# The output gate's projection of linear attention as a section of its own ahead of the mLSTM's fill

## The chip, the cores and the metric

The kernel runs on one core of a Trainium2 chip. The metric is the device time of one launch in microseconds; lower is better. The core has five engines with a queue each: TensorE (PE in the profile), VectorE (DVE), ScalarE (ACT), GpSimd (POOL) and SyncE (SP, which only issues transfers here).

## What is computed

Two layers act on a residual stream of 512 positions and 1024 features. Each layer adds half a SwiGLU, then a mixer of three parallel token mixers, then half a SwiGLU.

```python
z = h @ w_in + b_in                        # all projections of the mixer
o_a = gla_chunked(a_q, a_k, a_v, log_alpha)            # gated linear attention
o_a = rms_norm(o_a, gla_out_norm) * silu(a_r)          # a_r: its output gate
o_b = nsa_attention(b_q, ...)                          # sparse attention, 8 heads
o_c = mlstm_chunked(c_q, c_k, c_v, c_i, log_f) * sigmoid(c_o)
y = (sigmoid(gate_a) * (o_a @ w_branch[0]) + sigmoid(gate_b) * (o_b @ w_branch[1])
     + sigmoid(gate_c) * (o_c @ w_branch[2]))
x = x + y @ w_out
```

The change is about where the four tiles of `a_r` (128 features by 512 positions each) are projected.

## The kernel before

**Tiles, units, steps.** Activations lie with features on the partitions and the 512 positions along the free axis. Every float32 weight goes through three passes: a transfer on SP brings a unit (two weight tiles) into `raw`; ACT copies a tile rounded into `whi` (line 298, `split_tile`; line 289 in loops); POOL subtracts to get the rest into `wlo` (line 265). PE then does three matmuls for each 128 input features: `hhi,whi`, `hlo,whi`, `hhi,wlo`. These three are called a step here. A projection tile has 8 steps (lines 1191 to 1193), a tile of a combine unit 6 (lines 1247 to 1249). `whi` and `wlo` have two places, so that tile T+2 is split once PE has ended tile T. Semaphores carry it: `tile_done`, `hi_done`, `lo_done`, `raw_ready`, and `unit_free` for the PSUM banks.

**Sections and fills.** `SECTIONS` gives the order of the weights. The three token mixers have long chains of small operations on ACT and DVE. While these run, PE gets steps of a section that needs no result of theirs. A plan is a pair: at how many steps each slot begins, and at how many steps each tile ends. On PE `fill_group(n)` or `fill(name, n)` emits the steps of slot n. On ACT and DVE `fill` and `fill_group`/`fill_combine` stand at their own places n and handle the tiles that end at or before slot n (`ended`): ACT splits tile T+2 and, in a combine unit, makes the gate with a sigmoid (line 412, which needs another activation table than the exponentials do); DVE adds a bias (line 793) or multiplies the gate in (line 803), which also frees the unit's banks. All three engines take their queues in order.

**Sparse attention** has 16 groups m: `values(m)` ends group m; `scores(m + 1)` stands ahead of its slots. Group m works on m mod 4 + 1 blocks of 128 columns and has four slots q. In each, PE transposes a row of probabilities (line 1458), ACT copies it out of the one bank 6 into `prt` (line 504) and makes the exponentials of the next group (line 492), and PE's next transposes wait for that copy. The fill is plan `PM1`: 12 tiles, 96 steps, 16 of them in slots 0 to 3, 80 in the 64 slots of the groups: one step in slots q = 0, 1, 2 and two in q = 3.

**mLSTM** first has a head of eight slots (0 to 7): PE transposes eight tiles (line 1288), DVE does the gates' scans and four convolutions of four operations each (lines 1013 and 1016), ACT copies and applies Silu (lines 525 and 528). Line 1484 waits for the last Silu. Then come four heads h with slots 8 + 4h to 11 + 4h: PE makes four products, slots 8 + 4h and 9 + 4h, three products (lines 1495 to 1497), slot 10 + 4h, the sums (lines 1501, 1504), slot 11 + 4h. Line 1488 of the next head waits for DVE's chain behind line 1504 (`h_out`, line 1050, behind a reciprocal). The fill is plan `CB` on section `cb0`: 16 tiles of 6 steps, 96 steps, four in each slot. Linear attention comes after that with `cb1`.

## Time and profile before

| | us |
|---|---|
| median of 3 runs | 2916.95 |
| lowest and highest | 2909.89, 2918.77 |
| the profiled execution's own time | 2915.71 |
| its span, first to last instruction | 2913.9 |
| PE busy | 2749.6 (94%) |
| DVE busy | 1304.5 (45%) |
| POOL busy | 1069.6 (37%) |
| ACT busy | 1024.4 (35%) |
| mean granted PE clock, of full speed | 0.979 |

Busy times of matmuls overlap a little, as they are pipelined, so PE's share is not its distance from its peak. Most of PE's waits lie where the three token mixers run. The stretches of interest are, in layer 0, 587 to 722 us (the sparse attention's groups), 722 to 758 (the mLSTM's head) and 758 to 849 (its four heads), and in layer 1 the same some 1442 us later.

### The profile page before, as it was taken

Reading aid. Unit: us, or ns where it says so; the run is one execution under the profiler, and the core shown is the slowest. Engines: PE = TensorE matmul, PEld = TensorE weight load, DVE = VectorE, ACT = ScalarE, POOL = GpSimd, SP = SyncE. Lnnn points to the kernel's source line nnn. Section 1 sums busy time; section 2 is a strip of 40 time slices with the busy share of each in tenths; the row PEclk is TensorE's granted clock in tenths of the full one; section 3 lists DMA queues with packets and bytes.
Section 4 is the critical chain, followed back from the end, with each engine's and each line's share of the span. In section 5 each row is a group of like instructions: output and inputs, shape, how many; then the busy total and the mean of one; then the engine's idle time right before and its main releaser. Section 6 shows DMA issues by size and latency. Waiting matters only on the chain.

```text
span 2913.9 us, 36798 instructions
## 1 busy us (share of the span) xinstructions
PE 2749.6 (94%) x13092; PEld 2169.3 (74%) x13092; DVE 1304.5 (45%) x1596; ACT 1024.4 (35%) x1498; POOL 1069.6 (37%) x450
## 2 busy tenths in 40 slices
PE   6999999999988999999999999999998889999998
PEld 5888877766666787888878888767665667878887
DVE  6333353444655455332353333444454563653322
ACT  3222233555535433222232222244554454332221
POOL 3444444411222343444434444443112223444443
PEclk9999999999989999999999999999998999999999
DMA  3222222211111132223222222232011112222231
GB/s 134 89 99 103 99 87 97 100 45 34 53 45 44 66 108 92 88 100 114 89 73 101 96 100 92 87 108 87 30 44 44 55 44 76 101 92 99 88 119 68
DMA packets 36070, 239.54 MB, mean 82 GB/s; under 512 B 3952, under 2 KB 5232, under 8 KB 13936
## 3 DMA queue, kind: packets, MB, share of 16 engines
q1 hardware_dynamic: 32720, 232.80, 22.7%
q10 hardware_dynamic: 3232, 5.17, 0.5%
q8 instruction: 74, 1.21, 0.2%
q14 instruction: 44, 0.36, 0.0%
HBM read 234.81 MB, written 2.10 MB: 81 GB/s over the span
## 4 chain that ended last, share of the span: by engine, by line
issue 63%; POOL 24%; PE 11%; POOLq 1%; DVE 0%; DVEq 0%
POOL wlo L265 24%; PE bank L1191 4%; PE bank L1192 4%; PE bank L1193 4%; POOLq L264 1%; POOLq L260 1%; DVE hlo L689 0%; DVE x L759 0%; POOL selr L252 0%; DVE hhi L687 0%; POOLq L265 0%; POOLq L256 0%; POOL ones L249 0%; POOL onesm L250 0%; DVEq L759 0%
## 5 line engine op out<-in xcount | busy, mean ns | idle before, releaser
L265 POOL TENSOR_TENSOR wlo<-raw,whi 128x1024 fp32r<-128x1024 f32 (+2 forms) x440 | 1068.0, 2429 | 1825.2 <-ACT whi L298 926.1
L1191 PE MATMUL bank<-hhi,whi 128*128 128x512 f32 x1984 | 798.4, 402 | 48.3 <-POOL wlo L265 36.7
L1193 PE MATMUL bank<-hhi,wlo 128*128 128x512 f32 x1984 | 777.8, 392 | 0.0
L1192 PE MATMUL bank<-hlo,whi 128*128 128x512 f32 x1984 | 777.5, 392 | 0.0
L289 ACT ACTIVATE whi<-raw 128x1024 fp32r<-128x1024 f32 (+1 forms) x232 | 264.0, 1138 | 717.8 <-PE bank L1193 717.6
L1191 PEld LDWEIGHTS bank<-hhi,whi 128*128 128x128 f32 x1984 | 376.4, 190 | 137.9 <-issue 47.2
L1193 PEld LDWEIGHTS bank<-hhi,wlo 128*128 128x128 f32 x1984 | 375.5, 189 | 79.5
L1192 PEld LDWEIGHTS bank<-hlo,whi 128*128 128x128 f32 x1984 | 376.3, 190 | 75.0 <-issue 3.1
L746 DVE TENSOR_TENSOR tmp<-tmp,bank 128x512 f32<-128x512 f32 x80 | 55.0, 688 | 534.0 <-PE bank L1193 534.0
L1191 PE MATMUL bank<-uhi,whi 128*128 128x512 f32 x704 | 274.3, 390 | 0.0
L1193 PE MATMUL bank<-uhi,wlo 128*128 128x512 f32 x704 | 273.9, 389 | 0.0
L1192 PE MATMUL bank<-ulo,whi 128*128 128x512 f32 x704 | 273.9, 389 | 0.0
L298 ACT ACTIVATE whi<-raw 128x1024 fp32r<-128x1024 f32 (+2 forms) x176 | 173.2, 987 | 278.3 <-PE bank L1193 138.8
L736 DVE TENSOR_TENSOR ulo<-tmp,uhi 128x512 f32 (+1 forms) x88 | 212.6, 2415 | 10.1
L1247 PE MATMUL bank<-hhi,whi 128*128 128x512 f32 x384 | 165.9, 432 | 16.8 <-POOL wlo L265 16.6
L386 ACT ACTIVATE tmp<-bank 128x512 f32<-128x512 f32 x80 | 47.8, 597 | 362.1 <-PE bank L1193 347.8
L759 DVE SCALAR_TENSOR_TENSOR x<-bank,x 128x512 f32 x32 | 22.1, 692 | 319.2 <-PE bank L1193 319.2
L1248 PE MATMUL bank<-hlo,whi 128*128 128x512 f32 x384 | 156.3, 407 | 0.0
L689 DVE SCALAR_TENSOR_TENSOR hlo<-x,cur,hhi x48 | 153.5, 3198 | 6.2
L1249 PE MATMUL bank<-hhi,wlo 128*128 128x512 f32 x384 | 155.3, 404 | 0.0
L1191 PEld LDWEIGHTS bank<-uhi,whi 128*128 128x128 f32 x704 | 132.2, 188 | 28.6 <-issue 1.2
L1193 PEld LDWEIGHTS bank<-uhi,wlo 128*128 128x128 f32 x704 | 132.2, 188 | 27.7
(266 smaller groups left out, 3148.9 us busy)
## 6 DMA issues: line engine op xcount, KB each, us to landing
raw<-gu SPq DMA_DIRECT2D x88, 1024.0 KB, 4.8
raw<-dn SPq DMA_DIRECT2D x32, 1408.0 KB, 6.0
raw<-cb SPq DMA_DIRECT2D x48, 768.0 KB, 4.3
raw<-pM SPq DMA_DIRECT2D x16, 1024.0 KB, 4.7
raw<-cq SPq DMA_DIRECT2D x16, 1024.0 KB, 4.8
raw<-pA SPq DMA_DIRECT2D x12, 1024.0 KB, 4.7
raw<-wo SPq DMA_DIRECT2D x8, 1024.0 KB, 4.8
x<-xT ACTq DMA_DIRECT2D x4, 512.0 KB, 9.7
```

The lines of the kernel that those rows point to most:

```text
L265: pool.tensor_tensor(wlo[:, s, 0:w], raw[:, j, lo:lo + w], whi[:, s, 0:w].bitcast(f32), ALU.subtract).then_inc(sem["lo_done"], 1)
L289: A(whi[:, s, 0:w], raw[:, j, lo:lo + w], ACT.Copy).then_inc(sem["hi_done"], 1)
L298: A(whi[:, s, 0:(wa, wb)[s]], raw[:, u % 2, s * wa:s * wa + (wa, wb)[s]], ACT.Copy).then_inc(sem["hi_done"], 1)
L689: dve.scalar_tensor_tensor(hlo[:, c], x[:, c], gain, hhi[:, c].bitcast(f32), ALU.mult, ALU.subtract).then_inc(sem["pre_lo"], 1)
L736: dve.tensor_tensor(ulo[:, c], tmp[:, 2 + j], uhi[:, c].bitcast(f32), ALU.subtract).then_inc(sem["ulo_ready"], 1)
L746: dve.tensor_tensor(tmp[:, 2 + j], tmp[:, j], bank[2 * j + 1][:], ALU.mult).then_inc(sem["unit_free"], 1)
L1191: mm(outp, wh, mhi, start=start and k == 0, stop=False)
L1192: mm(outp, wh, mlo, start=False, stop=False)
L1193: i = mm(outp, wl, mhi, start=False, stop=stop and k == len(parts) - 1)
L1247: mm(outp, wh, mhi, start=k == (2 if s else 0), stop=False)
L1248: mm(outp, wh, mlo, start=False, stop=False)
L1249: i = mm(outp, wl, mhi, start=False, stop=bool(s) and k in (1, 5))
```

## The change

The last four of the twelve tiles of `pM1`, which are `a_r`, become section `pR`. The order of weights on SP, ACT and POOL is as it was. The sparse attention's 64 slots get 48 steps in place of 80: none in q = 0, one in q = 1, 2, 3. The mLSTM's 24 slots get 128 steps (four tiles of 8, then `cb0`'s sixteen of 6), 5 or 6 in each slot, in place of 96. No arithmetic is added or taken away.

```diff
-SECTIONS = [..., ("pM0", 2), ("cq", 8), ("pM1", 6), ("cb0", KD), ("cb1", KD),
+SECTIONS = [..., ("pM0", 2), ("cq", 8), ("pM1", 4), ("pR", 2), ("cb0", KD), ("cb1", KD),
...
-PM1 = ([4 * n if n < 4 else 16 + (n - 4) * 80 // 64 for n in range(69)], [KD * (i + 1) for i in range(12)])
+PM1 = ([4 * n if n < 4 else 16 + (n - 4) * 48 // 64 for n in range(69)], [KD * (i + 1) for i in range(8)])
+RCB = ([n * 128 // 24 for n in range(25)], [KD * (i + 1) for i in range(4)] + [4 * KD + 6 * (i + 1) for i in range(2 * KD)])
...
 # ACT: RCB's tiles
+                def fill_first(n):
+                    for T in ended(RCB, n):
+                        if T + 2 < len(RCB[1]):
+                            split_tile("pR", T + 2)
+                        if T >= 4 and T % 2:
+                            gate_unit(0)(T - 4)
...
-                split_tile("cb0", 0)
-                split_tile("cb0", 1)
+                split_tile("pR", 0)
+                split_tile("pR", 1)
...
-                    fill("cb0", CB, n, gate_unit(0))
+                    fill_first(n)
...
                 for h in range(NH):
                     fill("cb1", CB, h, gate_unit(1))
+                act.wait_ge(sem["unit_free"], me.at("unit_free", FIRST["pR"] + 2))
...
 # DVE
+                def fill_first(n):
+                    for T in ended(RCB, n):
+                        if T < 4:
+                            group_tile(FIRST["pR"] + T // 2, T % 2, MT_TILES - 4 + T)
+                        elif T % 2:
+                            combine_unit(0, T // 2 % 2, FIRST["cb0"] + T // 2 - 2, T // 2 - 2)
...
 # PE
+                def fill_first(n):
+                    at, ends = RCB
+                    for c in range(at[n], at[n + 1]):
+                        T = min(i for i, e in enumerate(ends) if c < e)
+                        u, s = FIRST["pR"] + T // 2, T % 2
+                        free = u - 1 if s == 0 else None
+                        if T < 4:
+                            step(2 * u, s, bank[2 * (u % 2) + s][:], hp, c % KD, free=free)
+                        else:
+                            gated(2 * u, u % 2, s, (c - 4 * KD) % 6, free=free)
...
-                        fill("cb0", n - 1)
+                        fill_first(n - 1)
...
-    arr["pM0"], arr["pM1"] = pm[:, 0:2], pm[:, 6:12]
+    arr["pM0"], arr["pM1"], arr["pR"] = pm[:, 0:2], pm[:, 6:10], pm[:, 10:12]
```

On PE, in the sparse attention's second group (two blocks), the first slot stood as follows: two transposes, a step, then the next two transposes and a step.

```order
L1458 MATMUL bank<-con,tmp 128x128 x2
L1191 MATMUL bank<-hhi,whi 128x512
L1192 MATMUL bank<-hlo,whi 128x512
L1193 MATMUL bank<-hhi,wlo 128x512
L1454 REGISTER_ALU
L1458 MATMUL bank<-con,tmp 128x128 x2
L1191 MATMUL bank<-hhi,whi 128x512
L1192 MATMUL bank<-hlo,whi 128x512
L1193 MATMUL bank<-hhi,wlo 128x512
```

With the change (its lines are numbered a little higher: 1488 is what was 1458, and 1209 to 1211 what was 1191 to 1193) the same place reads:

```order
L1488 MATMUL bank<-con,tmp 128x128 x2
L1484 REGISTER_ALU
L1488 MATMUL bank<-con,tmp 128x128 x2
L1209 MATMUL bank<-hhi,whi 128x512
L1210 MATMUL bank<-hlo,whi 128x512
L1211 MATMUL bank<-hhi,wlo 128x512
```

The first slot's step has gone, so that the second pair of transposes follows the first pair with nothing between. The last slot of the same group stood so, with two steps ahead of the values (line 1439):

```order
L1458 MATMUL bank<-con,tmp 128x128 x2
L1375 REGISTER_ALU
L1186 REGISTER_ALU
L1191 MATMUL bank<-hhi,whi 128x512
L1192 MATMUL bank<-hlo,whi 128x512
L1193 MATMUL bank<-hhi,wlo 128x512
L1191 MATMUL bank<-hhi,whi 128x512
L1192 MATMUL bank<-hlo,whi 128x512
L1193 MATMUL bank<-hhi,wlo 128x512
L1439 MATMUL bank<-prt,raw 64x128 x8
L1442 MATMUL bank<-tmp,vcm 64x128 x2
```

It now has one step there:

```order
L1488 MATMUL bank<-con,tmp 128x128 x2
L1209 MATMUL bank<-hhi,whi 128x512
L1210 MATMUL bank<-hlo,whi 128x512
L1211 MATMUL bank<-hhi,wlo 128x512
L1469 MATMUL bank<-prt,raw 64x128 x8
L1472 MATMUL bank<-tmp,vcm 64x128 x2
```

On DVE, in the mLSTM's head, the first convolution stood behind one multiplication of a gate (line 803), which reads PSUM:

```order
L1004 TENSOR_SCALAR zm<-zm 128x512
L1005 REGISTER_ALU
L802 REGISTER_ALU
L803 TENSOR_TENSOR y<-tmp,bank 128x512
L805 REGISTER_ALU
L1013 TENSOR_SCALAR tmp<-zm,cur 128x512
L1014 REGISTER_ALU
L1016 SCALAR_TENSOR_TENSOR tmp<-zm,cur,tmp 128x511
```

Now two bias additions stand there (line 794 is what was 793, 1031 and 1034 what was 1013 and 1016):

```order
L1022 TENSOR_SCALAR zm<-zm 128x512
L1023 REGISTER_ALU
L793 REGISTER_ALU
L794 TENSOR_SCALAR zm<-bank,cur 128x512
L793 REGISTER_ALU
L794 TENSOR_SCALAR zm<-bank,cur 128x512
L1031 TENSOR_SCALAR tmp<-zm,cur 128x512
L1032 REGISTER_ALU
L1034 SCALAR_TENSOR_TENSOR tmp<-zm,cur,tmp 128x511
```

One more addition stands behind the second convolution and one behind the third, where one multiplication stood behind the third. The multiplications move to the four heads.

## Rows read from the trace of the kernel before

**Rows 1.** Busy time by stretch (us; PE, PEld, DVE, ACT, POOL; granted clock, DMA share, GB/s).

```profile
587.20:722.30 135.10, 130.99 (x958) 89.20 (x956) 63.77 (x142) 69.62 (x197) 23.35 (x11) 0.99 0.11 36
722.30:757.80 35.50, 29.08 (x135) 22.18 (x133) 30.64 (x37) 19.97 (x28) 10.04 (x5) 0.95 0.20 67
757.80:782.00 24.20, 22.40 (x74) 14.90 (x74) 9.47 (x14) 14.67 (x23) 7.28 (x4) 0.86 0.10 33
782.00:842.00 60.00, 56.58 (x196) 38.88 (x196) 25.92 (x39) 21.78 (x38) 10.95 (x6) 0.89 0.16 53
```

**Rows 2.** What PE waited for, both layers (total us, times, longest).

```profile
PE bank L1488 <- DVE tmp L1050: 10.4, 6, 1.8
...
PE bank L1458 <- ACT prt L504: 6.4, 10, 1.0
```

**Rows 3.** Timeline of ACT in the sparse attention (start us, us long, instruction).

```profile
650.10 0.60 ACT L504 ACTIVATE prt<-bank 128x512 f32<-128x512 f32 x1 [0.46 <-PE bank L1458]
...
664.93 0.20 ACT L492 ACTIVATION_READ_ACCUMULATOR tmp<-bank,st 128x1 f32 x1
665.16 0.38 ACT L504 ACTIVATE prt<-bank 128x256 f32<-128x256 f32 x1
```

**Rows 4.** Timeline of PE in the sparse attention.

```profile
657.68 0.30 PE L1458 MATMUL bank<-con,tmp 128*128 128x128 f32 x1 [0.96 <-ACT prt L504]
...
664.71 0.41 PE L1458 MATMUL bank<-con,tmp 128*128 128x128 f32 x2
...
665.69 0.41 PE L1458 MATMUL bank<-con,tmp 128*128 128x128 f32 x2
...
667.49 0.77 PE L1439 MATMUL bank<-prt,raw 128*64 128x128 f32 x10
```

**Rows 5.** Timeline of PE, mLSTM of layer 0.

```profile
757.79 0.49 PE L1484 MATMUL bank<-rows,selr 64*128 64x512 f32 x1 [1.82 <-ACT zm L528]
...
768.79 0.91 PE L1495 MATMUL bank<-zm 64*128 64x384 f32 x2
...
770.29 0.50 PE L1247 MATMUL bank<-hhi,whi 128*128 128x512 f32 x1
...
773.14 2.32 PE L1501 MATMUL bank<-raw,zm 128*128 128x512 f32 x8
...
781.95 0.49 PE L1488 MATMUL bank<-rows,selr 64*128 64x512 f32 x1 [1.80 <-DVE tmp L1050]
```

**Rows 6.** Timeline of PE, mLSTM of layer 1.

```profile
2200.18 0.79 PE L1484 MATMUL bank<-rows,selr 64*128 64x512 f32 x1 [3.43 <-ACT zm L528]
...
2212.59 0.91 PE L1495 MATMUL bank<-zm 64*128 64x384 f32 x2
```

**Rows 7.** Timeline of DVE in the mLSTM of layer 0.

```profile
737.12 2.07 DVE L1004 TENSOR_SCALAR zm<-zm 128x512 f32<-128x512 f32 x1
...
739.84 0.42 DVE L1004 TENSOR_SCALAR zm<-zm 128x512 f32<-128x512 f32 x1
740.38 0.69 DVE L803 TENSOR_TENSOR y<-tmp,bank 128x512 f32<-128x512 f32 x1
...
741.81 2.32 DVE L1016 SCALAR_TENSOR_TENSOR tmp<-zm,cur,tmp 128x511 f32<-128x511 f32 x3
...
744.75 3.74 DVE L1016 SCALAR_TENSOR_TENSOR tmp<-zm,cur,tmp 128x511 f32<-128x511 f32 x3
...
772.65 0.69 DVE L803 TENSOR_TENSOR y<-tmp,bank 128x512 f32<-128x512 f32 x1
```

**Rows 8.** Timeline of POOL in the mLSTM of layer 0.

```profile
736.54 2.37 POOL L265 TENSOR_TENSOR wlo<-raw,whi 128x768 fp32r<-128x768 f32 x1 [2.73 <-ACT whi L298]
...
762.05 1.82 POOL L265 TENSOR_TENSOR wlo<-raw,whi 128x768 fp32r<-128x768 f32 x1 [10.25 <-ACT whi L298]
```

**Rows 9.** Timeline of ACT in the mLSTM of layer 0.

```profile
761.14 0.83 ACT L298 ACTIVATE whi<-raw 128x768 fp32r<-128x768 f32 x1
...
765.36 0.64 ACT L548 ACTIVATE tmp<-bank 128x512 f32<-128x512 f32 x1
```

More of the change, by code:

```diff
@@ L26 @@
 R_F, R_I, R_LR, R_G = 0, 32, 64, 96
-SECTIONS = [("gu0", KF), ("dn0", KD), ("pA", 6), ("pM0", 2), ("cq", 8), ("pM1", 6), ("cb0", KD), ("cb1", KD),
+SECTIONS = [("gu0", KF), ("dn0", KD), ("pA", 6), ("pM0", 2), ("cq", 8), ("pM1", 4), ("pR", 2), ("cb0", KD), ("cb1", KD),
             ("cb2", KD), ("wo", KD // 2), ("gu1", KF), ("dn1", KD)]
@@ L191, in build @@
             "cs_mm": 2, "cs_sub": 2, "cs_exp": 2, "cs_out": 2, "cs_t": 2, "cs_pt": 2,
-            "s_mm": 64, "s_max": 32, "s_exp": 64, "s_p": 64, "s_t": 64, "s_pt": 64, "pv": 16, "g_free": 12,
+            "s_mm": 64, "s_max": 32, "s_exp": 64, "s_p": 64, "s_t": 64, "s_pt": 64, "pv": 16, "g_free": 8,
             "o_hi": 12, "o_lo": 12,
@@ L293, in split_tile @@
                     u, s = FIRST[name] + T // 2, T % 2
-                    wa, wb = widths(name)
+                    wa, wb = widths(name) if name != "pR" or T < 4 else widths("cb0")
                     if s == 0:
@@ L532, in _ @@
                 for h in range(NH):
-                    fill("cb0", CB, 8 + 4 * h, gate_unit(0))
+                    fill_first(8 + 4 * h)
                     if h:
@@ L549, in _ @@
                     for n in range(1, 4):
-                        fill("cb0", CB, 8 + 4 * h + n, gate_unit(0))
-                fill("cb0", CB, 24, gate_unit(0))
+                        fill_first(8 + 4 * h + n)
+                fill_first(24)
                 split_tile("cb1", 0)
@@ L790, in fill_group @@
                     for T in ended(PM1, n):
-                        u, c = FIRST["pM1"] + T // 2, MT_TILES - 12 + T
+                        c = MT_TILES - 12 + T
                         dve.wait_ge(sem["tile_done"], me.at("tile_done", 2 * FIRST["pM1"] + T + 1))
@@ L1007, in _ @@
                 for n in range(4):
-                    fill_combine(0, n)
+                    fill_first(n)
                 for c in range(4):
@@ L1018, in _ @@
                         dve.wait_ge(sem["cv"], me.next("cv"))
-                    fill_combine(0, 4 + c)
+                    fill_first(4 + c)
                 dve.wait_ge(sem["rt_mm"], me.next("rt_mm"))
@@ L1022, in _ @@
                 for h in range(NH):
-                    fill_combine(0, 8 + 4 * h)
+                    fill_first(8 + 4 * h)
                     dve.wait_ge(sem["d_exp"], me.next("d_exp"))
@@ L1038, in _ @@
                     dve.wait_ge(sem["den_sum"], me.next("den_sum"))
-                    fill_combine(0, 9 + 4 * h)
-                    fill_combine(0, 10 + 4 * h)
+                    fill_first(9 + 4 * h)
+                    fill_first(10 + 4 * h)
                     dve.wait_ge(sem["den_mm"], me.next("den_mm"))
@@ L1054, in _ @@
                     dve.wait_ge(sem["h_gated"], me.next("h_gated"))
-                    fill_combine(0, 11 + 4 * h)
-                fill_combine(0, 24)
+                    fill_first(11 + 4 * h)
+                fill_first(24)
                 def out_low(b, first, tiles=range(4)):
@@ L1475, in _ @@
                 i.then_inc(sem["rt_mm"], 1)
-                fill("cb0", 7)
+                fill_first(7)
                 pe.wait_ge(sem["vm_ready"], me.at("vm_ready", 8))
@@ L1490, in _ @@
                     mm(bank[6][:], sel(h), rows[:, 1], start=True, stop=True).then_inc(sem["mm_mm"], 1)
-                    fill("cb0", 8 + 4 * h)
-                    fill("cb0", 9 + 4 * h)
+                    fill_first(8 + 4 * h)
+                    fill_first(9 + 4 * h)
                     pe.wait_ge(sem["d_exp"], me.next("d_exp"))
@@ L1497, in _ @@
                     mm(bank[4][:, 2 * P:3 * P], k[:, 3 * P:S], q[:, 3 * P:S], start=True, stop=True).then_inc(sem["sm_mm"], 1)
-                    fill("cb0", 10 + 4 * h)
+                    fill_first(10 + 4 * h)
                     for jt in range(NB):
@@ L1504, in _ @@
                     mm(bank[6][:], ones[:], tmp[:, 4], start=True, stop=True).then_inc(sem["den_mm"], 1)
-                    fill("cb0", 11 + 4 * h)
+                    fill_first(11 + 4 * h)
                 fill("cb1", 0)
```

## The prediction

> **What bounds the kernel now.** The page gives PE 94% of the span, so I looked for the stretches in which PE is not what ends last. The busy times by stretch show three of them [rows 1]. In the sparse attention PE is busy 130.99 of 135.10 us at a granted clock of 0.99. In the mLSTM's head it is busy 29.08 of 35.50 us; DVE, with 30.64 us, is the denser engine there. In the four heads PE is busy nearly throughout, but the granted clock is 0.86 and 0.89 of full speed. So the step that looks best placed today is one in the sparse attention, and the one that looks free is one in the mLSTM. The timelines say something else about the first.
>
> In the sparse attention I looked at ACT behind PE's transposes. ACT ends reading its accumulator at 665.13 and starts its next copy at 665.16 [rows 3]: it has no gap. PE's transposes follow each other in the same 0.98 us, from 664.71 to 665.69, with one step between [rows 4]. So slots q = 0 to 2 run at ACT's pace. The slot with two steps takes 1.80 us, from 665.69 to 667.49, 0.82 more [rows 4]; there PE ends last. With four blocks ACT falls idle for 0.46 us and then copies for 0.60 [rows 3]; PE's next transposes wait for that copy, which takes as long as the step does.
>
> In the mLSTM I looked at what PE waits for. Line 1488 waits for DVE's reciprocal chain 10.4 us in six waits [rows 2], 1.80 of them ahead of the second head [rows 5]. Line 1484 waits for DVE's convolutions through ACT's last Silu, 1.82 us in layer 0 and 3.43 in layer 1 [rows 5, 6]: DVE's chain, not PE's work, sets where the head ends.
>
> **Price of a step.** Four steps take 2.85 us, from 770.29 to 773.14 [rows 5], with some 0.12 of drain; another one beside them costs 0.68. The change takes 32 steps, 21.9 us a layer, from one place and puts them in the other. Transfers, splits and subtractions stay in their order on SP, ACT and POOL.
>
> **The sparse attention, a layer.** The 16 steps of q = 0 lie under ACT's work [rows 3, 4]: taking them away gives 0. With one block the copy is short and PE's next transposes could start a little sooner, but ACT's exponentials would still hold the ones after. The second step of q = 3 is worth 0.68, bounded above by the 0.82 of the two-step slot. With four blocks ACT's last copy then comes a little after the step, and I count 0.55. Twelve times 0.68 and four times 0.55 are 10.4. What could be late next is DVE's scaling of the next group; the values and scores stand between, and the copies are all that PE waits for there now [rows 2]. Then the splits: where ACT splits a weight between two copies, PE waits, 0.96 us in one case [rows 4] and 6.4 us in ten over both layers [rows 2]. By the plan six of eight splits a layer fall between copies; after it two of four. Of 3.2 us a layer, two waits of 0.85 stay: gain 1.5. Sum: -11.9 a layer, -23.8 for both.
>
> **The mLSTM's head, a layer.** Ten more steps, 6.8 us, enter the eight slots, in which PE is now idle for 6.4 us [rows 1]. The end is DVE's. It loses two multiplications (0.69 each [rows 7]) and gets four bias additions that read PSUM too; at the same 0.69 that is +1.4. POOL decides the rest. While POOL subtracts from 736.54 to 738.91 [rows 8], DVE's line 1004 takes 2.07 us, elsewhere 0.42; three operations of line 1016 take 3.74 in place of 2.32 [rows 7]. The passes move: if line 1004 is no longer hit, the head ends 1.65 earlier (-0.3); if one more operation is hit, 1.65 later (+3.0). I take +1.3. The Trainium skill, "SBUF — State Buffer", section "SBUF: two separate sides", says that DVE and GpSimd share a pair of ports as an exclusive lock for a whole instruction. The stretched line 1004 agrees; by that rule the head's bound is set by whose instruction starts first, which no sum foretells.
>
> **First head.** ACT does four sigmoids, then the split. It ends 761.97 [rows 9] and POOL 763.87 [rows 8], 6.1 us after line 1484. Now that tile begins two steps into slot 8 in place of four, so PE waits for it: a wait of 0.7 to 2.4 us by the clock. Six steps later comes the next tile, whose split stands behind the exponentials: ACT ends them at 766.00 [rows 9], 8.2 after line 1484; 0.83 and 1.82 more [rows 8, 9] are 11.1. Three more steps end at 13.2. Before, line 1495 stood 11.0 behind line 1484 in layer 0 [rows 5] and 12.4 in layer 1 [rows 6]. So +2.2 and +0.8. Slot 10 has one step more (0.68), and its fourth begins the third combine unit, whose banks DVE frees only behind line 803, 4.55 us after line 1495 [rows 5, 7]. PE is there at 3.6: a new wait of 1.0. That is +1.7 in each layer. Slot 11's two extra steps lie under the 1.80 that line 1488 waits.
>
> **Later heads.** Heads 1 to 3 get 12 steps a layer that nothing covers, 8.2 us, and one each in slots 15 and 19 that the wait covers. The waits at line 1488 shrink from 1.80 to 0.4, 1.1 and 1.1. The granted clock was 0.89 over these 60 us [rows 1]; a clock at either 1.2 or 2.4 GHz makes that 13.2 us at 1.2, which cost 6.6. I take it that PE's shorter waits no longer bring it down: -6.6. Net +1.6. The last slot's two steps lie under DVE's work for linear attention; I put 0.4 on it.
>
> **Sum.** Layer 0: 1.3 + 2.2 + 1.7 + 1.6 + 0.4 = 7.2. Layer 1: 5.8. Together +13.0, against -23.8: -10.8 us. The profiled execution took 2915.71, 1.2 below the median of 2916.95. From 2915.7 this gives 2904.9, from the median 2906.2. I say 2905.
>
> **Rivals.**
> - *The clock keeps falling between heads*, chance 0.17. For it: it fell behind waits of 1.8 us with PE at work on both sides. Against it: the waits shrink by 0.7 to 1.4. Price 6.6 a layer: 2918, no change. The Trainium skill, "TensorE: Matmul & The Clock Gate", section on HAM oscillation, tells of kernels in which a wait ahead of each block of work puts the clock down each time. The granted 0.89 here agrees; by that rule, if 1.1 us is still enough, the time is this rival's.
> - *DVE's chain in the head gets off lightly*, 0.15. Line 1004 is not hit (-1.6 a layer), PE hardly waits at line 1484 and the clock in the first head, 0.86 over 24.2 us [rows 1], comes back to full, 3.4 us at most, about half of it behind the new wait for the split. That is about -7 more: 2898.
> - *Supply of weights*, 0.12. Tiles now follow each other with less other work between, and splits stand behind ACT's exponentials in each head. If the third and fourth head wait like the first, 2 us and the clock's 1.7 for two heads and both layers give +15 at worst, +7 likely: 2912. In the third head the tile is needed about 6.0 us behind line 1488 and I find it ready at 5.2; that is close.
> - *The other side: the second step of q = 3 is covered as well*, 0.07. If what follows it (values, scores, the next first transposes) is really held by ACT's exponentials and DVE's scaling, then only 3.0 of the splits come back against +13.0: 2926, slower. The kernel ends slower at all once less than half of the 10.4 is won, and by over 0.3% only if next to nothing of it is. Against it: the two-step slot is 0.82 longer than its neighbours.
> - The forecast, 0.49, with its own range of 2899 to 2910.
>
> **Numbers.** A measurement of this kernel tells about 0.3%, 8.7 us, from no change: faster is below 2908. The forecast gives 0.41 of its chance to faster and 0.08 to same; the light chain 0.15 faster; the clock 0.14 same and 0.03 slower; supply 0.04 faster, 0.07 same, 0.01 slower; the other side 0.07 slower. Sum 0.60, 0.29, 0.11. The range 2894 to 2918 reaches to the light chain below and to the middle of the clock's case above.
>
> **What would show it.** Right: slots of q = 3 at about 1.1 us and q = 0 to 2 as before; the sparse attention's 135.1 us at about 123; line 1484 within 1 to 3 us of its old distance from the first transposes; line 1488 waiting 0.4 to 1.1; a clock near 1.0 over heads 1 to 3; new waits for POOL in slot 8 and for DVE in slot 10 of the first head. Wrong: q = 0 slots that get shorter, a clock that stays at 0.89, or waits for `wlo` in every head.

## The result and the profile after

The changed kernel takes 2919.05 us in the median of ten runs (2912.86 to 2922.51); the kernel before, run ten times beside it, 2911.36. The ratio is 1.0026 with a 95% interval of 1.0014 to 1.0038: some 7.7 us slower, where 10.8 us faster was forecast. (The median of 2916.95 that the forecast started from was that of three runs; ten runs of the same kernel spread from 2903.74 to 2918.77.) The profiled execution took 2918.60 us over a span of 2916.8. Two single executions in the slow state, of 15,378 us (the kernel before, beside e5, e6 and e7) and of 11,066 us (e9), count in no ratio.

The four stretches that answer to [rows 1], in layer 0 of the kernel after (the columns are those of [rows 1]):

```profile
585.90:710.20 124.30, 112.29 (x862) 74.81 (x860) 63.27 (x138) 65.83 (x192) 13.22 (x6) 0.97 0.07 26
710.20:749.20 39.00, 35.19 (x166) 28.04 (x162) 34.56 (x39) 16.07 (x24) 12.80 (x6) 0.96 0.18 61
749.20:777.30 28.10, 24.27 (x92) 16.03 (x91) 9.39 (x13) 15.84 (x25) 9.13 (x5) 1.00 0.18 57
777.30:842.40 65.10, 63.06 (x237) 45.01 (x238) 27.36 (x41) 25.12 (x42) 16.45 (x9) 0.95 0.17 61
```

The sparse attention, 135.10 us before, takes 124.30. The head is 3.5 us longer, with DVE at 34.56 us in place of 30.64. The clock is back in the first head (1.00 for 0.86), but only at 0.95 in the later ones. What PE waited for, both layers, beside [rows 2]:

```profile
PE bank L1488 <- ACT prt L513: 11.1, 17, 0.8
PE bank L1318 <- ACT zm L534: 5.7, 2, 2.9
PE bank L1518 <- DVE tmp L1068: 4.9, 6, 1.1
PE bank L1265 <- DVE y L813: 1.5, 2, 0.8
```

Line 1518 (1488 before) waits 4.9 us in place of 10.4; line 1318 (1288) has a wait of 2.9 us in each layer for ACT's copy, and the wait for DVE's line 813 is new.

All kernels of this study, by the starts of the same matmuls in their timelines, layer 0 / layer 1, in us. "Sparse" runs from the first transposes (line 1458 before) to the product for alpha (line 1451), which stands ahead of the last group; "head" from there to line 1484, so that it holds the sparse attention's last group too; "four heads" to the last head's line 1501; "LA 2nd half" is linear attention's second pair of heads, in which no kernel changes anything. The time is the median; each ratio goes by runs of the kernel before beside that kernel.

| kernel | steps in the mLSTM | sparse | head | four heads | LA 2nd half | time | ratio to before |
|---|---|---|---|---|---|---|---|
| before | 96 | 124.9 / 125.7 | 45.7 / 45.6 | 81.6 / 83.0 | 45.1 / 45.2 | 2911.4 | |
| after | 128 | 113.6 / 113.8 | 49.8 / 49.8 | 90.5 / 90.6 | 48.0 / 48.0 | 2919.1 | 1.0026 |
| e1, narrow passes | 128 | 113.9 / 113.5 | 46.0 / 46.0 | 88.5 / 87.0 | 48.1 / 48.1 | 2905.0 | 0.9979 [0.9967, 0.9990] |
| e2, waits covered | 128 | 113.7 / 113.7 | 49.8 / 49.8 | 83.5 / 83.5 | 48.1 / 48.1 | 2905.6 | 0.9978 [0.9965, 0.9991] |
| e3, one unit, even | 112 | 116.6 / 116.4 | 48.7 / 48.3 | 82.8 / 82.3 | 47.9 / 48.2 | 2906.1 | 0.9983 [0.9971, 0.9996] |
| e4, one unit, placed | 112 | 117.2 / 116.3 | 48.5 / 48.4 | 74.0 / 74.0 | 47.8 / 45.9 | 2888.4 | 0.9921 [0.9900, 0.9942] |
| e5, two units, placed | 128 | 114.0 / 113.5 | 52.8 / 52.8 | 80.1 / 80.1 | 47.9 / 45.5 | 2898.6 | 0.9956 [0.9941, 0.9971] |
| e6, none moved, placed | 96 | 125.6 / 124.9 | 46.7 / 46.6 | 69.8 / 71.4 | 48.1 / 45.2 | 2891.9 | 0.9928 [0.9913, 0.9944] |
| e8, as e4, splits last | 112 | 111.3 / 111.5 | 47.7 / 47.5 | 74.0 / 74.6 | 45.9 / 48.1 | 2877.5 | 0.9873 [0.9854, 0.9892] |
| e9, as e8, head changed | 112 | 112.2 / 111.4 | 51.1 / 50.5 | 75.8 / 75.4 | 47.5 / 48.2 | 2885.4 | 0.9896 [0.9877, 0.9916] |
| e10, two units, splits last | 128 | 112.0 / 112.6 | 52.9 / 52.9 | 83.3 / 82.0 | 47.2 / 45.5 | 2902.9 | 0.9972 [0.9959, 0.9985] |
| e11, as e6, splits last | 96 | 118.7 / 118.7 | 48.8 / 48.8 | 71.4 / 71.4 | 47.6 / 47.5 | 2882.6 | 0.9899 [0.9880, 0.9918] |

Against before, the kernel after wins 11.4 and 12.0 us in the sparse attention and loses 4.1 and 4.1 in the head (0.6 of it in the sparse attention's last group, 3.5 behind it), 8.9 and 7.6 in the four heads, 1.4 and 1.4 from there to linear attention, and 2.9 and 2.9 in linear attention's second half. The first question was why the head and the heads cost more than forecast, the second where the last 2.9 come from.

DVE in the head of the kernel after, and POOL beside it:

```profile
711.72 2.65 DVE L994 SCALAR_TENSOR_TENSOR tmp<-z 4x512 f32<-4x512 f32 x1
...
724.48 3.30 DVE L1017 TENSOR_TENSOR rows<-tmp,rows 4x1024 fp32r<-4x1024 f32 x1
...
731.35 1.56 DVE L1031 TENSOR_SCALAR tmp<-zm,cur 128x512 f32<-128x512 f32 x1
...
735.89 3.79 DVE L1034 SCALAR_TENSOR_TENSOR tmp<-zm,cur,tmp 128x511 f32<-128x511 f32 x3
...
741.04 3.79 DVE L1034 SCALAR_TENSOR_TENSOR tmp<-zm,cur,tmp 128x511 f32<-128x511 f32 x3
```

```profile
709.12 4.71 POOL L266 TENSOR_TENSOR wlo<-raw,whi 128x1024 fp32r<-128x1024 f32 x2 [37.37 <-ACT whi L299]
724.27 2.42 POOL L266 TENSOR_TENSOR wlo<-raw,whi 128x1024 fp32r<-128x1024 f32 x1 [10.44 <-ACT whi L299]
730.22 2.41 POOL L266 TENSOR_TENSOR wlo<-raw,whi 128x1024 fp32r<-128x1024 f32 x1 [3.53 <-ACT whi L299]
736.75 2.38 POOL L266 TENSOR_TENSOR wlo<-raw,whi 128x768 fp32r<-128x768 f32 x1 [4.12 <-ACT whi L299]
```

The first three long instructions of DVE start inside one of POOL's passes and end 0.3 to 1.1 us behind it. Line 1017 works on four partitions; it starts 0.21 us behind the start of POOL's pass of 724.27 and ends 1.09 behind its end, so that of its 3.30 us some 2.2 are the rest of the pass. Twice a pass falls into the three operations of a convolution, which then take 3.79 in place of 2.32, as in [rows 7]. Line 1004, which took 2.07 us there, is not hit now.

PE in the same place has one long wait at the head's start and none at its end:

```profile
718.82 0.66 PE L1318 MATMUL bank<-con,zm 128*128 128x128 f32 x4 [2.88 <-ACT zm L534]
...
749.24 0.49 PE L1514 MATMUL bank<-rows,selr 64*128 64x512 f32 x1
```

```profile
748.56 0.63 ACT L537 ACTIVATE zm<-tmp 128x512 f32<-128x512 f32 x1 [2.57 <-DVE tmp L1034]
```

ACT's last Silu ends at 749.19, and PE is busy up to line 1514 at 749.24: both end together, where PE had waited 1.82 us before [rows 5].

### The profile page after: what moved, and what is told of

It is laid out like the page before. It is cut to its first block, busy times and chain, and to the rows that moved or that the text cites. A ratio compares the mean times of both kernels' runs of the same rounds, so it can differ in the third digit from the quotient of the medians.

```text
span 2916.8 us, 36796 instructions
## 1 busy us (share of the span) xinstructions
PE 2741.5 (94%) x13092; PEld 2168.2 (74%) x13092; DVE 1313.8 (45%) x1596; ACT 1018.0 (35%) x1492; POOL 1072.4 (37%) x450
## 3 DMA queue, kind: packets, MB, share of 16 engines
q8 instruction: 74, 1.21, 0.2%
## 4 chain that ended last, share of the span: by engine, by line
issue 63%; POOL 24%; PE 11%; POOLq 1%; DVE 0%; DVEq 0%
POOL wlo L266 24%; PE bank L1209 4%; PE bank L1211 4%; PE bank L1210 4%; POOLq L265 1%; POOLq L261 1%; DVE hlo L699 0%; DVE x L769 0%; POOL selr L253 0%; DVE hhi L697 0%; POOLq L266 0%; POOLq L257 0%; POOL ones L250 0%; POOL onesm L251 0%; DVEq L769 0%
## 5 line engine op out<-in xcount | busy, mean ns | idle before, releaser
L1209 PEld LDWEIGHTS bank<-hhi,whi 128*128 128x128 f32 x1984 | 376.3, 190 | 139.9 <-issue 48.4
L387 ACT ACTIVATE tmp<-bank 128x512 f32<-128x512 f32 x80 | 47.9, 599 | 357.3 <-PE bank L1211 343.1
L1210 PEld LDWEIGHTS bank<-ulo,whi 128*128 128x128 f32 x704 | 132.2, 188 | 27.5
```

Of the source, the lines that this page charges most:

```text
L1209: mm(outp, wh, mhi, start=start and k == 0, stop=False)
L1210: mm(outp, wh, mlo, start=False, stop=False)
```

## The experiments

**e1: is the head longer because of POOL's passes?**

```diff
-                                pool.tensor_tensor(wlo[:, s, 0:w], raw[:, j, lo:lo + w],
-                                                   whi[:, s, 0:w].bitcast(f32), ALU.subtract).then_inc(sem["lo_done"], 1)
+                                n_ = 64 if name == "pR" else w
+                                pool.tensor_tensor(wlo[:, s, 0:n_], raw[:, j, lo:lo + n_],
+                                                   whi[:, s, 0:n_].bitcast(f32), ALU.subtract).then_inc(sem["lo_done"], 1)
```

> The kernel after, in which GpSimd's subtraction for the four tiles of the output gate works on 64 columns only (the rest of wlo of these tiles is left out, so part of the projection's correction is missing); everything else stays. Theory A, the mLSTM's head is longer by 4.1 us a layer because VectorE's operations (the 2.65, 3.30 and 1.56 us that stood at 0.73, 1.22 and 0.55 before) lie under GpSimd's longer passes: these three operations fall back to their short times, the 2.88 us wait for ACT's copy of zm shrinks by 2 us or more and the low clock behind it goes; the head gets 3 to 4.5 us shorter in each layer, and the whole kernel 6 to 9 us faster than the kernel after, about level with the kernel before. Rival B, the head is longer because TensorE has ten more steps in it and is itself the bound: the operations may get shorter, but the distance from line 1484's matmul of alpha to line 1514 changes by less than 1 us, and so does the time.

DVE in the same place (lines stand one lower):

```profile
712.32 0.67 DVE L995 SCALAR_TENSOR_TENSOR tmp<-z 4x512 f32<-4x512 f32 x1
...
723.14 1.21 DVE L1018 TENSOR_TENSOR rows<-tmp,rows 4x1024 fp32r<-4x1024 f32 x1
...
730.86 0.55 DVE L1032 TENSOR_SCALAR tmp<-zm,cur 128x512 f32<-128x512 f32 x1
731.45 2.32 DVE L1035 SCALAR_TENSOR_TENSOR tmp<-zm,cur,tmp 128x511 f32<-128x511 f32 x3
```

The three operations fall to 0.67, 1.21 and 0.54 to 0.55 us, and the head from 49.8 to 46.0 in both layers, with the same 42 steps in it. PE's wait of 2.9 us for ACT's copy is 0.89 now, and the low clock that followed it (3.4 us at half the clock, so 1.7 us lost) is gone. These two make up the 3.8 us. The wait hangs on the first of the three operations alone, the one of 2.65 us, since ACT takes its queue in order and waits for its result ahead of the copy. The other two lengthen the chain to the last Silu: in e1 it ends at 744.15, and PE, still busy, reaches its product 2.1 us later, at 746.21. The kernel is 14 us faster than the one after, more than the 6 to 9 that theory A gave: the first head also got 2.0 us shorter, since its first split, behind the last Silu, is ready sooner against PE (the wait for `wlo` in slot 8 went from 2.28 to 0.31). Theory A stands: the passes are what lengthened the head. Rival B falls as a reason for the 4.1 us, but with the passes gone PE's own steps set the head's end.

**e2: does the clock fall because of the waits?**

```diff
-RCB = ([n * 128 // 24 for n in range(25)], ...
+RCB = ([0, 5, 10, 16, 21, 26, 32, 37, 42, 47, 52, 57, 64, 69, 74, 78, 85, 90, 95, 99, 106, 112, 117, 122, 128], ...
```

> The kernel after with the same 128 steps in the mLSTM, 42 in its head and 86 in its four heads as before, but slots 11, 15 and 19, behind which line 1518 waits for VectorE, get seven steps in place of 6, 5 and 5, taken from slots 10, 13 to 14 and 17. Theory A, the clock falls behind the waits of 0.45 to 1.11 us: the waits fall below 0.3 us, the clock stays at full speed over heads 1 to 3, and a layer's four heads get 4 to 5 us shorter (1.5 to 2 of the waits themselves, 3.4 of the clock); 8 to 10 us faster than the kernel after. Rival B, the clock falls for what these matmuls are (64 partitions, float32), whatever the waits: only the waits are won, 1.5 to 2 us a layer, 3 to 4 us in all, and low stretches stand where they stood.

The stretch of the later heads:

```profile
777.30:837.30 60.00, 60.00 (x240) 43.37 (x240) 28.29 (x42) 24.72 (x42) 16.49 (x9) 1.00 0.21 66
```

PE is busy without a gap and the clock is full over 60 us, where it was 0.95 after and 0.89 before [rows 1]; line 1518 waits no more. The four heads take 83.5 us in place of 90.5, by moving five steps (from slots 8, 14, 17 and 18, not quite those that the expectation names). Of these 7 us, 0.45, 0.89 and 1.11 are the waits and 0.7 the one for DVE's line 813, of which 0.08 is left. Of the rest, some 3.9 us, the clock explains 3.3: 0.95 over 65 us in the row of the kernel after is 6.5 us at 1.2 GHz, half of it lost. Theory A stands, at 7 us a layer in place of its 4 to 5; the time is 13.5 us better than after. The Trainium skill, "TensorE: Matmul & The Clock Gate", section on HAM oscillation, lays such a loss to a wait that recurs ahead of each block of work. The rows agree in kind; but the waits in the page's example are of some 3 to 5 us, and here 0.89 and 1.11 us were enough.

Both waits stand in PE's timeline of the kernel after. Behind the first, matmuls of 512 columns that take 0.39 us at full clock take 0.63:

```profile
800.03 0.50 PE L1518 MATMUL bank<-rows,selr 64*128 64x512 f32 x1 [0.89 <-DVE tmp L1068]
...
801.97 0.63 PE L1267 MATMUL bank<-hhi,wlo 128*128 128x512 f32 x1
...
824.33 0.49 PE L1518 MATMUL bank<-rows,selr 64*128 64x512 f32 x1 [1.11 <-DVE tmp L1068]
```

The traces of all kernels together bear it out, and show its limit. Ahead of the second, third and fourth head PE waited 0.89 us or more in 32 cases; in 27 the granted clock fell right behind the wait. In 52 cases it waited 0.5 us or less, and the clock never fell. The five exceptions (one in e1, three in e3, one in the kernel before as delayed for e7) had waits of 0.89 to 1.80 us like the others, so a wait of this length makes the fall likely and not certain.

**e3: are steps in the slots q = 0 free?** One unit (16 steps) stays where it was: `pR` is the last unit of `pM1`, the sparse attention has one step in each slot.

```diff
-SECTIONS = [..., ("pM1", 4), ("pR", 2), ...
+SECTIONS = [..., ("pM1", 6), ...
+FIRST["pR"] = FIRST["pM1"] + 5
-PM1 = ([4 * n if n < 4 else 16 + (n - 4) * 48 // 64 for n in range(69)], [KD * (i + 1) for i in range(8)])
-RCB = ([n * 128 // 24 for n in range(25)], [KD * (i + 1) for i in range(4)] + [4 * KD + 6 * (i + 1) for i in range(2 * KD)])
+PM1 = ([4 * n if n < 4 else 16 + (n - 4) for n in range(69)], [KD * (i + 1) for i in range(10)])
+RCB = ([n * 112 // 24 for n in range(25)], [KD * (i + 1) for i in range(2)] + [2 * KD + 6 * (i + 1) for i in range(2 * KD)])
...
```

The lines left out carry the smaller number of tiles through ACT, DVE, PE and the host's arrays.

> Only one of the two units of the output gate's projection is moved: the sparse attention keeps 64 steps in its 64 slots, one in each, and the mLSTM gets 112, four or five in each slot. Theory A, a step in the slots q = 0 costs nothing because ScalarE ends last there: the sparse attention from its first transposes to the matmul of alpha takes 123.5 to 125 us in layer 0, within 1 us of the kernel after, while the mLSTM loses half of what the kernel after lost, 6 to 8 us a layer; in all 3 to 5 us a layer better than before, 6 to 10 us faster than the kernel before. Rival B, each step in q = 0 costs its 0.68: the sparse attention takes 5 to 6 us more a layer than the kernel after, and the whole is level with the kernel before or slower.

PE and ACT in a group of three blocks (line 1489 transposes, 514 copies, 300 splits):

```profile
633.98 0.55 PE L1489 MATMUL bank<-con,tmp 128*128 128x128 f32 x3
...
635.20 0.52 PE L1489 MATMUL bank<-con,tmp 128*128 128x128 f32 x3
...
637.19 0.52 PE L1489 MATMUL bank<-con,tmp 128*128 128x128 f32 x3 [0.77 <-ACT prt L514]
...
638.38 0.52 PE L1489 MATMUL bank<-con,tmp 128*128 128x128 f32 x3
...
639.52 1.53 PE L1470 MATMUL bank<-prt,raw 128*64 128x128 f32 x24
```

```profile
634.56 0.49 ACT L514 ACTIVATE prt<-bank 128x384 f32<-128x384 f32 x1 [3.72 <-PE bank L1489]
...
635.61 1.06 ACT L300 ACTIVATE whi<-raw 128x1024 fp32r<-128x1024 f32 x1
636.56 0.49 ACT L514 ACTIVATE prt<-bank 128x384 f32<-128x384 f32 x1
```

Slot q = 0, with a step, takes 1.22 us, exactly what it takes in the kernel after without one (602.18 less 600.96 there). The step is free, as theory A says. But the sparse attention is 3.0 and 2.7 us longer than after, not within 1. The rows show the reason: slot q = 1 takes 1.99 us in place of 1.19, since the split of 1.06 us stands between two copies. Six slots a layer have it (1.92 to 2.00 us), at 0.8 to 0.95 each, where the kernel after has two such places. The time, 2906.1, is 5.7 us better than before, just short of theory A.

**e4 and e6: steps placed under waits, with one unit moved and with none.** e4 is e3 with another list of slots; e6 is the kernel before with a plan of its own for `cb0`. In steps per slot:

```
e4  head 8 5 5 5 4 4 5 5   heads 4 4 4 6 | 4 4 4 6 | 4 4 4 6 | 5 4 4 4
e6  head 7 4 4 3 3 3 4 4   heads 4 3 3 6 | 4 3 3 6 | 4 3 3 6 | 4 4 4 4
```

> As the run with one unit moved, but its 112 steps in the mLSTM are placed by hand under the waits: eight in slot 0, four or five in the others of the head, six in slots 11, 15 and 19 and four in the rest. Theory A, steps are free under waits and the clock falls behind waits: sparse attention as in the kernel after (11 us a layer less than before), head of the mLSTM within 1 us of before, line 1518's waits below 0.5 us and few low stretches of the clock in the heads, which are then 2 us longer to 2 us shorter than before; 14 to 24 us faster than the kernel before. Rival B, the clock falls whatever the waits, and the supply of weights makes new waits: 5 us a layer longer in the mLSTM than by theory A, no better than the even spread.

> The kernel before, nothing moved, with only the 96 steps of its mLSTM placed: seven in slot 0, three or four in the rest of the head (32 in all as before), six in slots 11, 15 and 19, three or four in the others of the heads. Theory A, placement and move are two gains that add: line 1488's waits of 1.80, 1.63 and 1.80 fall to 0.3 to 0.5 us, two of the three low stretches behind them go, the sparse attention stays at 125 us; 5 to 8 us a layer, in all 10 to 16 us faster than the kernel before, which leaves 8 to 13 us of the 23 that one unit placed gained to the move. Rival B, placement alone is the whole gain: 2888 to 2892. Rival C, without more steps than waits the clock falls all the same: 3 to 6 us faster only.

The waits of e4 and of e6 that answer to [rows 2] (lines stand one lower than after, and than before):

```profile
PE bank L1519 <- DVE tmp L1069: 2.4, 6, 0.5
PE bank L1319 <- ACT zm L535: 1.7, 2, 0.8
```

```profile
PE bank L1489 <- DVE tmp L1051: 2.4, 6, 0.5
PE bank L1289 <- ACT zm L526: 8.8, 2, 4.4
```

In both, line 1488's waits are 0.2 to 0.5 us, and the clock stays full in heads 1 to 3. e4 is 23.4 us faster than before, inside theory A's 14 to 24, but its parts came out otherwise: the sparse attention is 8 to 9 us shorter than before and not 11, the head 2.8 us longer and not within 1, and the four heads 7.6 and 9.0 us shorter where at most 2 were expected. That the sum fits is luck. And e6 is 19.9 faster with nothing moved, more than theory A gave and the upper edge of its rival B, although its head has a new wait of 4.4 us: nine steps put into other slots of the mLSTM are worth five sixths of e4's gain. The price of the move itself, e6 against e4, is -8.5 us a layer in the sparse attention, +1.8 in the head and +3.4 in the heads, on the mean.

**e5: two units, placed** (head 9 6 5 5 5 5 6 5, heads 5 5 4 7 | 5 5 4 7 | 5 5 4 7 | 5 5 4 5).

> The kernel after, both units moved, with its 128 steps of the mLSTM placed by hand: nine in slot 0, five or six in the rest of the head (46 in place of 42), seven in slots 11, 15 and 19, four or five in the others. Theory A, each place has a price of its own: the sparse attention stays 2.5 to 3.5 us a layer shorter than with one unit moved, but 16 more steps stand in the mLSTM, of which some 6 find a wait; so the mLSTM is 6 to 8 us a layer longer than in the run with one unit placed, and the whole 5 to 10 us slower than that run's 2888.4: 2893 to 2898, some 15 to 20 us faster than the kernel before. Rival B, PE's work in the mLSTM is now dense and its clock full, so that nothing else is lost, and the whole comes out at or below 2888.

At 2898.6 it is 10.2 us slower than e4, just past theory A's range, and 20 faster than after. Rival B falls. Its head takes 52.8 us: PE waits 3.08 us there for a `wlo` whose split stands behind a Silu, and the Silu waits for DVE. In the form that was tested, the second unit doesn't pay.

**e7: does linear attention's second half depend on where the clock's low stretches fall?** The kernel before, with the last head's product for the denominator made three or six more times; each was executed once.

```diff
+                    for _ in range(3 if h == 3 else 0):
+                        mm(bank[6][:], ones[:], tmp[:, 4], start=True, stop=True)
                     mm(bank[6][:], ones[:], tmp[:, 4], start=True, stop=True).then_inc(sem["den_mm"], 1)
```

> The kernel before with the matmul of the denominator of the last head made three more times ahead of itself, in each layer; it only delays what follows by 1 to 3 us. Theory A, the second half of linear attention (from line 1534 of the second pair to the second pair's gate sums, 45.15 us in both layers of the kernel before and 48.0 to 48.1 in the kernel after) is longer only where the clock's low stretches happen to fall: with another start it takes 45 to 48.5 us, different from 45.15 in at least one layer of the two delayed kernels. Rival B, the kernel after and its relatives do something else there (other buffers, other order of splits): with the code of before it stays at 45.1 to 45.3 us whatever the start.

> As the run before it, with six repeated matmuls in place of three, a delay of 2 to 6 us. Theory A: the second half of linear attention takes 45 to 48.5 us, and in the two delayed kernels together at least one layer is off 45.15 by over a microsecond. Rival B: 45.1 to 45.3 us in every layer.

The second half of before and of after (layer 0), then both layers of the first delayed kernel and layer 0 of the second:

```profile
933.47:978.62 45.15, 42.11 (x278) 32.80 (x279) 32.46 (x56) 25.78 (x37) 12.89 (x7) 0.96 0.20 71
```

```profile
935.09:983.12 48.03, 45.13 (x277) 35.19 (x278) 30.92 (x56) 25.79 (x37) 12.78 (x7) 0.90 0.20 67
```

```profile
934.78:979.98 45.20, 42.22 (x278) 32.83 (x279) 32.48 (x56) 25.79 (x37) 12.92 (x7) 0.96 0.21 71
2369.95:2416.79 46.84, 42.34 (x278) 33.13 (x278) 32.47 (x56) 25.80 (x37) 12.96 (x7) 0.96 0.21 69
```

```profile
939.94:988.02 48.08, 45.15 (x277) 35.19 (x278) 30.98 (x56) 25.79 (x37) 12.79 (x7) 0.90 0.20 67
```

The instructions are the same in all five rows. With another start the code of before takes 45.20, 46.84 and 48.08 us (48.06 in layer 1 of the second kernel). At 45.2 the granted clock is 0.96, at 48.1 it is 0.90: of 45.15 us 3.6 at 1.2 GHz, of 48.03 us 9.6, and half of the difference is the 3.0 us. Rival B falls. The 2.9 us a layer that the kernel after loses here are no work of the change; they come with where the clock stood. The 46.84 came at 0.96 too. Its 1.6 us are a wait: at 2375.75 PE waits 1.62 us for DVE's line 1116, ahead of line 1539 (1537 before). In the row of 45.20 the low clock lies just there (the first products of the stretch take 2.08 us in place of 1.13) and covers that wait; in layer 1 it comes 39 us into the stretch, with nothing to cover. The same happens to the heads: layer 1 of this kernel, with the code, the steps and the waits of before, takes 78.2 us for its four heads, where the other layers with that code take 81.6 to 83.0. The clock's chance moves a stage of this kernel by 3 to 5 us.

**e8: splits behind the copy of slot q = 3.**

```diff
-PM1 = ([4 * n if n < 4 else 16 + (n - 4) for n in range(69)], ...
+PM1 = ([4 * n if n < 4 else min(17 + (n - 4), 80) for n in range(69)], ...
```

> The run with one unit placed, with one change: the sparse attention's first slots take 17 steps in place of 16 and its last slot none, so that the tiles end one slot earlier and ScalarE's splits stand behind the copy of slot q = 3, where TensorE has the values and the next scores to do, and not between the copies of q = 0 and q = 1. Theory A, in the run with one unit the price of the sparse attention was the splits between copies (six slots of 1.92 to 2.00 us in place of 1.05 to 1.19) and nothing else: all six fall back, the sparse attention takes 111.5 to 113 us a layer in place of 117.2 and 116.3, and the kernel 8 to 11 us less than the run with one unit placed, 2878 to 2881 us. Rival B, a split behind the last copy holds up the exponentials, the scaling and the next group's first slot instead: the gaps from values to the next transposes grow by what the slots win, and the time stays within 2 us.

The same group as shown for e3, and a split of this kernel:

```profile
631.21 0.55 PE L1489 MATMUL bank<-con,tmp 128*128 128x128 f32 x3
...
632.43 0.52 PE L1489 MATMUL bank<-con,tmp 128*128 128x128 f32 x3
...
633.62 0.52 PE L1489 MATMUL bank<-con,tmp 128*128 128x128 f32 x3
...
634.81 0.52 PE L1489 MATMUL bank<-con,tmp 128*128 128x128 f32 x3
...
635.96 1.53 PE L1470 MATMUL bank<-prt,raw 128*64 128x128 f32 x24
```

```profile
643.52 0.60 ACT L514 ACTIVATE prt<-bank 128x512 f32<-128x512 f32 x1 [0.46 <-PE bank L1489]
...
644.36 1.05 ACT L300 ACTIVATE whi<-raw 128x1024 fp32r<-128x1024 f32 x1
```

All four slots take 1.15 to 1.22 us, and the group's gap behind the values is 2.65 us as before. The sparse attention takes 111.3 and 111.5 us, less than in the kernel after although it has 16 steps more. Theory A stands; the time is just below its 2878 to 2881. 2877.5 us is the best of all: 1.27% faster than before.

**e9 and e10: the same with the head's steps moved, and with two units** (e9: head 8 5 5 5 5 6 6 2, one step more than e8 has there, taken from slot 20; e10: head 8 6 6 6 6 6 6 2, heads as e5, and `PM1` so that the six tiles end in slot q = 2 and their splits stand behind the copy of q = 3, in groups 2, 5, 7, 10, 13 and 15).

> As the run before it, and the steps of the mLSTM's head placed so that its fourth tile ends in slot 4 and the next two in slots 5 and 6 (8, 5, 5, 5, 5, 6, 6 and 2 steps in place of 8, 5, 5, 5, 4, 4, 5 and 5): ScalarE then meets each split one Silu earlier. Theory A, the head is held up by that split, for which TensorE waited 2.13 us in slot 6 since it stood behind a Silu that waited for VectorE: the wait goes, the head gets 1 to 2.5 us shorter a layer, 2 to 5 us in all. Rival B, VectorE's chain alone sets the head's end: the wait moves to line 1514's matmul behind the last Silu, and the head stays within 0.5 us.

> Both units moved, placed by hand, with both remedies: the tiles of the sparse attention end so that every split stands behind a copy of slot q = 3, and the head's 46 steps are placed 8, 6, 6, 6, 6, 6, 6 and 2. Theory A, with 16 steps fewer in the sparse attention, which are free there once the splits are out of the way, and 16 more in the mLSTM, where some 5 are free, the second unit does not pay: the sparse attention takes 111.5 to 113 us a layer, no less than with one unit, and the kernel is 10 to 16 us slower than the run with one unit and the same remedies, about 2889. Rival B, the sparse attention gets shorter still by 2 us or more a layer, and both come out equal within 3 us.

e9 answers neither theory: the head gets 3.4 and 3.0 us longer. The wait in slot 6 had already gone in e8, and line 1515's matmul now waits 5.18 us. DVE in e9's head:

```profile
736.47 3.79 DVE L1035 SCALAR_TENSOR_TENSOR tmp<-zm,cur,tmp 128x511 f32<-128x511 f32 x3
740.38 0.69 DVE L814 TENSOR_TENSOR y<-tmp,bank 128x512 f32<-128x512 f32 x1
...
741.90 3.79 DVE L1035 SCALAR_TENSOR_TENSOR tmp<-zm,cur,tmp 128x511 f32<-128x511 f32 x3
...
746.40 3.89 DVE L1035 SCALAR_TENSOR_TENSOR tmp<-zm,cur,tmp 128x511 f32<-128x511 f32 x3
750.41 0.69 DVE L814 TENSOR_TENSOR y<-tmp,bank 128x512 f32<-128x512 f32 x1
```

Three of four convolutions lie under a pass of POOL here, two in e8, and a second multiplication (line 814) stands ahead of the head's end: with more steps so early a second combine unit ends inside the head. e10 is 17.4 us above e9, its sparse attention at 112.0 and 112.6 no shorter than with one unit, its head 52.9. Theory A's direction holds, at a larger size: it had 10 to 16 us, and about 2889.

**e11: was anything to be moved?** e6 with e8's remedy.

> The run with nothing moved and the mLSTM placed, with one change: the 96 steps of the sparse attention are placed so that every split stands behind a copy of slot q = 3 (16 slots of two steps, in and ahead of the groups 2, 7, 14 and 15, all others one, the last none). It is the control of the best run so far, 2877.5 us, in which one unit is moved. Theory A, moving one unit pays by itself: 16 second steps cost 0.55 to 0.7 us each here, about 10 us a layer over the 111.4 us of that run, so the sparse attention takes 120 to 123 us; the mLSTM is about 5 us a layer shorter without the 16 steps; in all 2884 to 2889 us, 7 to 11 us slower than the best run and 3 to 8 us faster than the run with nothing moved and splits between copies. Rival B, the splits were all that a step too many cost: the sparse attention takes 112 to 116 us, and the kernel 2870 to 2878, so that nothing had to be moved at all.

The sparse attention takes 118.7 us, 7.4 over e8: a second step costs 0.46 us on the mean, less than the 0.55 to 0.7 expected. Neither theory's range for the sparse attention was met. The four heads are 2.6 to 3.2 us shorter than e8's, the head 1.1 to 1.3 longer. The median of 2882.6 is 5.1 above e8's; the two ratios' intervals overlap, but 7.4 and 7.2 us for the sparse attention stand in the trace. That trace is of e11's slowest execution, 2890.7 us, 8.1 above its median, so its stages together overstate the difference. Moving one unit is worth some 5 us here; placement, in the mLSTM and of the splits, some 30.

## Why the prediction was wrong

**The sparse attention was right, near enough**: -10.8 and -11.4 us over all its sixteen groups against -11.9 (-11.4 and -12.0 up to the product for alpha, and +0.6 in the last group). In a group of two blocks the last slot, 1.80 us in [rows 4], takes 1.04 after:

```profile
595.46 0.41 PE L1488 MATMUL bank<-con,tmp 128*128 128x128 f32 x2
...
596.43 0.41 PE L1488 MATMUL bank<-con,tmp 128*128 128x128 f32 x2
...
597.47 0.77 PE L1469 MATMUL bank<-prt,raw 128*64 128x128 f32 x10
```

The slot ahead of it stays at 0.97, and e3 shows that a step in q = 0 is free. What was not foreseen: the four products of 16 partitions ahead of the last group are now followed by a low clock (in that group, slots of 2.16 and 1.83 us where 1.41 stands in e3), which gave back 1.2 us. Why it falls there stays open.

**The head was mis-sized**: +3.5 in each layer behind the last group, where +1.3 was taken from a range of -0.3 to +3.0. The bias additions were counted well (0.75 each). Line 1004 is no longer hit, as one end of the range had it. What failed is the other end, "if one more operation is hit": the passes for `pR` are 1024 columns wide in place of 768 and lie elsewhere, and they reach three operations that ran free before, two of them short ones on four partitions that were not looked at. "The end is DVE's" also failed in part. The first of the three holds up PE itself, through ACT's copy, by a wait of 2.9 us with a low clock behind it, a path that the forecast did not have, and from there PE's steps run without a gap to the head's end. e1 takes these passes away, and 3.8 us come back, all of it. By the Trainium skill, "SBUF — State Buffer", section "SBUF: two separate sides", whichever starts first, a DVE operation with two SBUF inputs or a GpSimd operation, holds the shared ports for its whole instruction; line 1017, with two such inputs and 3.30 us, its own 1.21 and the rest of the pass, agrees.

**The first head was right** (+3.9 and +2.6 against +3.9 and +2.5), with the two waits that it named. The three products of line 1495 come 13.2 us behind line 1484, as forecast, and the slots up to the sums take 1.7 more. That the clock was full here (1.00 for 0.86) gave nothing: PE waited 2.28 us for its split instead, the top of the 0.7 to 2.4 foreseen.

**The later heads failed in one step**, "I take it that PE's shorter waits no longer bring it down: -6.6". The steps and waits came as forecast (+8.3 against +8.2 without the clock; waits of 0.45, 0.89 and 1.11 against 0.4, 1.1 and 1.1), but the clock gave back only half of the 6.6: waits of 0.89 and 1.11 us still brought it down, twice a layer. So the three heads are +5.0 in place of +1.6. This was the rival to which 0.17 was given, in its place and with its mechanism, at half its price; e2 shows it, as covering those waits brings 7 us a layer and a clock of 1.00. **The last slot's two steps** were mis-sized: +0.4 was put on them, as lying under DVE's work, and the stretch grew by 1.4, twice the 0.68 of a step. PE waits behind them for the next section's `wlo`, 3.96 us for 3.48 before, so nothing was covered. Together the forecast of +2.0 a layer became +6.4.

**Linear attention's second half** was not in the sum at all. Its +2.9 a layer is the clock's, shown by e7; why the low stretches fall as they do in a given start stays open. Elsewhere in the program the profiled execution of after was 6.6 us shorter than that of before, in stretches that no change touched: 9.5 us lost in the two mixers became 2.9 of span. More than half of it, 3.7 us, lies between the two mixers, at a granted clock of 1.00 for 0.99.

The miss is 18.5 us between the medians and 13.7 between the profiled executions (2904.9 forecast from 2915.7, 2918.6 measured), and only the latter can be shared out. The sparse attention has 1.6 of it, the head 4.5, the later heads with what follows 8.8, linear attention's second half 5.8, less some 7 where nothing was changed. The first three are in the main mechanisms of the change; the last two come with where the clock stood and aren't its work.

## What to carry to other kernels

Price a filler step by the engine that ends last in its slot, and then look at what rides on the step: here a tile's end sends a split to ACT, and whether that split stood between two copies or behind the last one was worth 5 to 6 us a layer, about as much as eight steps. Cover every wait of PE, those of a microsecond too, before moving work between stages: nine steps put into other slots of the mLSTM gave 20 us, the place of the splits some 9 more, moving a unit some 5. And where DVE's chain bounds a stage, count POOL's passes beside each of its instructions, the small ones as well, since one of 0.7 us can wait out a pass of 2.4.

## What the runs showed of the hardware

A DVE instruction on four partitions took 3.30 us in place of 1.21 beside a POOL pass of 2.42. The granted clock fell behind waits of 0.89 and 1.11 us with PE at work on both sides, and stayed full over 60 us without a gap; of 32 waits of 0.89 us or more ahead of a head 27 were followed by a fall, of 52 of at most 0.5 us none. The same 278 matmuls took 45.2 us at a granted clock of 0.96 and 48.1 at 0.90, with nothing changed but what delayed their start.
